# The order of VectorE's scaled copies in the two gating stages of a hybrid decoder step

## What is computed

```python
for i in range(DEPTH):                       # DEPTH = 2
    ...
    h = h + mix                              # convolution, or attention
    h = h + hier_moe(rmsnorm(h, norm_ffn[i]), ...)
    h = h + (p[i] @ ple_w_in[i]) * jax.nn.sigmoid(rmsnorm(h, ple_g[i]) @ ple_w_gate[i])
return rmsnorm(h, norm_final), ...
```

## Time and profile before

| | |
|---|---|
| median of 3 runs | 787.07 us (785.09 to 787.7) |
| the profiled execution, its own time | 784.27 us |
| its span, from the first to the last instruction | 782.6 us |
| TensorE busy | 728.6 us, 93% of the span |
| VectorE busy | 339.5 us, 43% |
| ScalarE busy | 208.0 us, 27% |
| granted TensorE clock, mean | 0.98 |
| read from HBM | 262.69 MB |

### The profile page before, as it was taken

The page is one execution under the profiler, slowest core; times in us unless marked ns, Lnnn a source line. Parts: engine busy times, 40 slices in busy tenths (PEclk is TensorE's granted clock), DMA queues, the critical chain, the costliest instruction groups (busy, mean ns, idle before and its releaser), DMA issues.

```text
span 782.6 us, 16338 instructions
## 1 busy us (share of the span) xinstructions
PE 728.6 (93%) x6286; PEld 523.4 (67%) x6286; DVE 339.5 (43%) x1001; ACT 208.0 (27%) x511; POOL 55.0 (7%) x99
## 2 busy tenths in 40 slices
PE   9999999999999779899899999999999998698994
PEld 7886677756666546568676657777766665365582
DVE  2687724533333223225446866245233333133246
ACT  2200333412222111142225744034221122011332
POOL 1501000000000000000043540000000000000000
PEclk9999999999999989999999999999999999799997
DMA  9977994999999999999458784999999999999801
GB/s 342 390 228 215 338 421 156 386 425 424 423 425 424 423 426 425 409 421 420 179 184 278 261 246 167 426 427 378 415 412 419 428 424 423 424 425 412 353 2 57
DMA packets 48912, 271.16 MB, mean 346 GB/s; under 512 B 6960, under 2 KB 17408, under 8 KB 28608
## 3 DMA queue, kind: packets, MB, share of 16 engines
q1 hardware_dynamic: 41520, 258.50, 81.3%
q10 hardware_dynamic: 4416, 6.86, 2.6%
q0 software_dynamic: 2896, 4.72, 2.2%
HBM read 262.69 MB, written 3.88 MB: 341 GB/s over the span
## 4 chain that ended last, share of the span: by engine, by line
PE 41%; DMA 13%; issue 13%; SPq 7%; DVE 4%; POOLq 2%; ACT 1%; POOL 1%; DVEq 0%
PE bank L831 11%; DMA ring<-in_moe_w_gate_up 9%; PE bank L787 7%; PE bank L860 5%; PE bank L667 5%; SPq L2414 5%; DMA arena<-in_moe_w_down 4%; PE bank L874 4%; SPq L2410 2%; POOLq L2301 2%; PE bank L804 1%; PE bank L594 1%; PE bank L754 1%; PE bank L1176 1%; PE bank L896 1%
## 5 line engine op out<-in xcount | busy, mean ns | idle before, releaser
L831 PE MATMUL bank<-ring,arena 128*32 128x256 f32 x1088 | 121.9, 392 | 3.9 <-DMA arena<-in_moe_w_gate_up 3.9
L667 PE MATMUL bank<-arena,ring 128*128 128x264 f32 (+1 forms) x440 | 103.4, 390 | 3.8 <-DVE arena L1733 3.8
L667 PE MATMUL bank<-xn_sq,ring 128*128 128x264 f32 x448 | 101.2, 386 | 0.0
L667 PEld LDWEIGHTS bank<-arena,ring 128*128 128x128 f32 x440 | 83.3, 191 | 21.3 <-DVE arena L1733 4.6
L667 PEld LDWEIGHTS bank<-xn_sq,ring 128*128 128x128 f32 x448 | 85.0, 190 | 15.3 <-issue 0.8
L787 PEld LDWEIGHTS bank<-arena 128*128 128x128 f32 x768 | 87.9, 192 | 8.3 <-issue 8.3
L1569 DVE TENSOR_TENSOR arena<-arena,bank 128x128 f32<-128x128 f32 x34 | 9.8, 288 | 188.4 <-ACT arena L2048 188.4
L787 PE MATMUL bank<-arena 128*128 128x128 f32 (+1 forms) x768 | 91.2, 277 | 0.0
L831 PEld LDWEIGHTS bank<-ring,arena 128*32 128x32 f32 x1088 | 61.6, 113 | 27.1 <-issue 10.7
L874 PE MATMUL bank<-arena 128*128 128x264 f32 x256 | 63.6, 393 | 2.9 <-issue 2.9
L1587 DVE TENSOR_TENSOR hT<-hT,bank 128x264 f32<-128x264 f32 x144 | 60.5, 428 | 10.8 <-PE bank L874 5.2
(11 more groups left out here) (296 smaller groups left out, 943.1 us busy)
## 6 DMA issues: line engine op xcount, KB each, us to landing
ring<-in_moe_w_gate_up SPq DMA_DIRECT2D x28, 2048.0 KB, 20.9
ring<-in_stream SPq DMA_DIRECT2D x34, 1024.0 KB, 15.3
ring<-in_moe_w_down SPq DMA_DIRECT2D x26, 1024.0 KB, 21.1
arena<-in_moe_w_down SPq DMA_DIRECT2D x26, 1024.0 KB, 21.6
arena<-in_moe_w_gate_up SPq DMA_DIRECT2D x12, 2048.0 KB, 21.4
xn_sq<-in_moe_w_gate_up SPq DMA_DIRECT2D x10, 2048.0 KB, 21.5
spare<-in_moe_w_gate_up SPq DMA_DIRECT2D x8, 2048.0 KB, 25.6
ring<-in_moe_w_gate_up SPq DMA_DIRECT2D x8, 1024.0 KB, 27.7
```

The lines of the kernel that those rows point to most:

```text
L667: t = mm(ps[:, 0:cols], lhs(k), rhs(k), start=(k == 0), stop=(k == n - 1))
L831: t = mm(bank[2 + r][p0:p0 + U, 0:F].rearrange("p (c f) -> p c f", c=2), x, w[i][:, :, k * F + c * P:k * F + (c + 1) * P], start=(k == 0), ...
```

## The change

VectorE's scaled copy of chunk m + 1 is issued at the start of step m, ahead of the square's addition, the product, the addition and the copy of chunk m, for m = 0 to 4. Step 0 begins with the scaled copies of 0 and 1, steps 1 to 4 with those of 2 to 5, step 5 has none, steps 6 and 7 have their own, as before. It is done in both layers, and nothing else is changed: the same 8 scaled copies, the same two halves of `sgp`.

```diff
+AHEAD = 5
...
+                def scaled(m):
+                    key = ("pg", l, m)
+                    ps = arrive(dve, key)
+                    v.tensor_tensor(sgp[:, m % 2, :], ps[:, 0:T], rstd[:], ALU.mult).then_inc(is_free(key), 1)
+
...
                 for m in range(KD):
                     if l and m == 3:
                         out_of_line()
-                    key = ("pg", l, m)
-                    ps = arrive(dve, key)
-                    v.tensor_tensor(sgp[:, m % 2, :], ps[:, 0:T], rstd[:], ALU.mult).then_inc(is_free(key), 1)
+                    if m not in range(1, AHEAD + 1):
+                        scaled(m)
+                    if m < AHEAD:
+                        scaled(m + 1)
                     if 1 < m <= ADDED[name][1] + 1:
                         add_square(name, m - 1)
```

## The result

The changed kernel takes 776.8 us by the median of 4 runs (776.59 to 777.54), the kernel before 787.38 us beside it (4 runs). The ratio is 0.9872, with a 95% interval of 0.9851 to 0.9894. Measured again in another group of runs it was 0.9891 (0.9871 to 0.9910). By these two ratios the change is worth 10.1 us (8.3 to 11.7) and 8.6 us (7.1 to 10.1); the forecast was 9.1.

What follows compares the result with a forecast made beforehand. VectorE's chain, though 43% busy, was taken to bound both gating stages. Layer 0's 5.8, layer 1's 3.0 and 0.3 sum to 9.1 us (7.2 to 9.4): 775.2 profiled, plus 2.80 gives 778.0 median, range 775.5 to 782.0.

Steps and rivals of the forecast that it cites:

- The bound and its chain: Gating stages: VectorE's chain via ScalarE bounds; moving scaled copies cuts the step from 2.78 to 1.91 us, then TensorE bounds.
- the DMA wait at m = 2: Layer 0: ScalarE's DMAs after its third sigmoid hold the next square 1.85 us; forecast to remain, from an earlier time.
- The distances between neighbours: VectorE start-to-start distances from the trace; two scaled copies in a row taken as 0.35 us, other end 0.43.
- TensorE behind layer 0, 5.8 us: Attention's second chunk full at 380.6 instead of 386.44 us: 4.2 from VectorE done earlier, 1.6 clock; bounds 4.2 to 6.0.
- That it reaches the end: After layer 0's gating, all that follows, expert stage included, shifts by the whole 5.8 us; lower end 0.
- rival 1: Layer 1's byte-bound expert stream ends when it did before; only layer 1's 3.3 us stay, 783.8 us; chance 0.10 with parts.
- the forecast row of the key loads' wait: Between 382 and 531 us: TensorE's longest wait is 1.4 us, for key loads whose issue GpSimd begins after a TensorE chunk.
- Layer 1, 3.3 us: Layer 1's gating to the root: last scaled copy 3.0 us earlier, plus 0.3 for clock, bounds 0 and 0.4.
- Rival 2: ScalarE: early copy's sigmoid stands behind the former square, period stays near 2.78; about 1 us gained, 786; chance 0.05.
- Rival 3: Earlier attention in layer 0 waits for query weights not landed; slower from a landing at 397 us on; chance 0.03.
- The exclusion: VectorE: an early scaled copy waiting for its chunk (0.4 us once, chunk 5 in layer 1) can't make the end later.
- a later period above 2 us without a wait for a bank: VectorE's gating steps: one of the listed signs that would show the prediction wrong.

## Why the prediction was right

**The bound and its chain.** VectorE's chain was the bound of both stages and TensorE's last chunk is now. Forecast starts of the scaled copies in layer 0 were 0, 0.35, 2.13, 3.69, 6.45, 8.36, 12.00 and 15.45 us. Measured: 0, 0.34, 2.13, 3.67, 6.44, 8.33, 11.96 and 15.45. The period of 1.91 us came as 1.89, and the DMA wait at m = 2 remained (scaled copy 4 at 6.44).

**The distances between neighbours.** They were the one thing that the trace of before didn't show for two scaled copies. I took 0.35 and they start 0.34 apart at durations of 0.43. Full durations between neighbours would have put scaled copy 7 at 15.8 us and the last gain copy 0.4 later; they came at 15.45 and 17.96. The sentence that the prediction took from the Trainium skill (VectorE: DVE Perf Modes, The DRAIN you can't avoid), that the next op waits for the pipe to empty, goes on in the same passage: a next op that is not held starts earlier. The prediction left that out, and so was wrong to say that the skill speaks against overlap. The rows here agree with the fuller passage, taking independent neighbours as not held: they start 0.34 to 0.35 us apart, or 0.27 behind a gain copy, which is less than they last, and dependent ones 0.46 to 0.47.

**TensorE behind layer 0, 5.8 us.** 4.2 by the stalls and 1.6 by the clock were forecast. The last gain copy came at 17.96 instead of 22.19 us after the first scaled copy, 4.2; the clock's part was isolated at 1.6 by filling the stalls. Second chunk 23.58 against 23.5 forecast.

**That it reaches the end.** Layer 0 alone gives 5.8 us of the program (0.9926), and putting TensorE back takes it away. The forecast held, and rival 1 (swallowed by the expert stream) falls; in the pair of traces the lead of 3.7 us behind the key loads' wait is still 3.7 at layer 1's first scaled copy (748.67 against 752.38), so the expert stage took none of it. I had allowed for no loss on the way, and the forecast row of the key loads' wait, 1.4 us, was in the earlier trace rows: it varies from 1.04 to 2.59 us between the traces of this study, and with the clock behind it the pair of traces lost 2.7 us there. Between the medians no loss shows that these runs could tell from none.

**Layer 1, 3.3 us.** 3.0 for the last scaled copy was exact. The rest was 0.3 with bounds of 0 and 0.4, and the trace pair gave 0.5: from the end of the last square to the root 767.22 - 766.41 = 0.81 us against 1.35. The bound of 0.4 was too low, but the term isn't a constant of the kernel before either. In the other three traces whose layer 1 is untouched the same distance was 1.59, 1.58 and, with fills at the keys, 774.27 - 773.47 = 0.80 us. So this part is gained only in executions where the clock would have been down there. Nor is it shown to reach the end: where the root was late by it the span ended 8.1 to 8.2 us behind the root, in the ten other traces 8.4 to 8.9, and from the end of the last square to the end of the span all thirteen lie between 9.2 and 9.9. For the end of the span the term may as well be nothing. By the ratio layer 1 gives 2.9 us.

**Rival 2** (the sigmoid behind the square on ScalarE keeps the period at 2.78) falls with the period of 1.89. **Rival 3** (query weights not landed) falls: TensorE's row of the second chunk runs on from 376.36 without a wait, and its waits from 380 to 740 us (those of 0.3 us and more) name no load ahead of L668, the line of the projections' chunks. **The exclusion** of a loss by the early copy's own wait held at five copies (0.49 us once, nothing at the end), and the seven copies show the point from which it does cost: 2.1 us. One sign of being wrong was worded too wide: "a later period above 2 us without a wait for a bank" is met by the forecast's own walk, which has 2.76 us at the DMA wait and a step 6 as before; the trace has them too (3.67 to 6.44, and 2.50 us from scaled copy 6 to its gain copy).

**The number.** Forecast 778.0, measured 776.8 and in the second group 777.4. In the chances 0.82 + 0.09 was a slip: two thirds of rival 1's 0.10 make 0.07, so "faster by over 0.3%" should have stood at 0.89. The offset from the profiled execution to the median, 2.8 us for the kernel before, is -0.7 for the changed one (777.54 profiled, 776.8 median): the profiled execution of before was shorter than all of its runs, and that of after longer than its others. The difference of the two profiled spans, 6.7 us, would have been a poor measure of the change.

## What to carry to other kernels

An engine that is 43% busy can be the bound of a stage by a chain that goes over another engine and back; what shortens it is the next step's independent work put into the wait, and the gain ends where the feeder's last piece arrives, which a walk through the starts found to 0.04 us in the changed kernel and to 0.16 with four copies. Run ahead no further than the feeder keeps up: four copies were enough, seven gave 2.1 us back, since what stands behind a waiting instruction waits too. Short stalls of TensorE ahead of its own work can cost more than their length: here 1.6 us by the clock on top of 4.2. But judge a single wait from several executions.

## What the runs showed of the hardware that I had not expected

The same wait, for the same loads in the same kernel, was 2.45 us in one execution of the changed kernel and 1.50 in another. Behind waits of 2.37, 2.45 and 2.59 us the granted clock had fallen (0.58 to 0.70 in the stretch from 458 to 462 us, in three of the traces); behind waits of 1.04 to 1.99 us, in seven others without products in the wait, it was 1.00. Behind two stalls of 1.74 and 2.07 us with two records between them it had fallen in the kernel before (0.69); behind a single one of 1.96, with two copies ahead, it had not. And the products of constants that kept it up cost nothing measurable in a wait, while they were worth 1.5 us at the stalls of layer 0, which stand alike in all three traces of that order (second chunk at 29.39 to 29.48 us), and nothing that these runs can tell at the key loads' wait, which differs from trace to trace.
